# Sums over later keys in a stick-breaking attention: two fp32r passes over a split softplus in place of one native 32 bit pass

## What is computed

```
z = (q . k) / 8                                   # per head, query t, key s
log_beta = log_sigmoid(z);  log_fail = -softplus(z) where s < t, else 0
survive[t, s] = sum of log_fail[t, j] over the keys j later than s
A[t, s] = exp(log_beta[t, s] + survive[t, s]) where s < t, else 0
o = A v
```

## Time and profile before

| | |
|---|---|
| time, median of 3 runs | 875.36 us (873.93 to 876.03) |
| profiled execution: time, span | 875.22 us, 873.3 us |
| TensorE busy | 844.2 us, 97% of the span |
| VectorE busy | 613.9 us, 70% |
| ScalarE busy | 489.5 us, 56% |
| granted TensorE clock, mean | 0.99 |

### The profile page before, as it was taken

How to read it: one execution, slowest core, us unless ns; L and a number is a source line. 1 busy time by engine, 2 the same in 40 slices (tenths; PEclk the granted TensorE clock), 3 DMA queues, 4 the chain that set the end, 5 groups by cost and what they waited for, 6 DMA issues and landing times.

```text
span 873.3 us, 16776 instructions
## 1 busy us (share of the span) xinstructions
PE 844.2 (97%) x6768; PEld 805.1 (92%) x6768; DVE 613.9 (70%) x1004; ACT 489.5 (56%) x814; POOL 145.8 (17%) x151
## 2 busy tenths in 40 slices
PE   7999999999999999999999998899999999999996
PEld 6999999999999989999999988799999999878886
DVE  6646887886666686776764588877797696567754
ACT  6346456455444575555564457768767564345554
POOL 0000000000000333333331121634324010000002
PEclk9999999999999999999999999799999999999999
DMA  9654424335566534555566524544545375653331
GB/s 338 205 158 140 139 98 169 122 125 180 181 190 184 178 97 152 185 180 185 190 193 205 180 88 134 184 153 150 167 148 164 106 235 180 186 168 111 110 95 49
DMA packets 39853, 139.81 MB, mean 160 GB/s; under 512 B 4432, under 2 KB 5600, under 8 KB 39648
## 3 DMA queue, kind: packets, MB, share of 16 engines
q1 hardware_dynamic: 37728, 135.71, 48.8%
q10 hardware_dynamic: 2048, 3.02, 1.0%
HBM read 137.65 MB, written 1.06 MB: 159 GB/s over the span
## 4 chain that ended last, share of the span: by engine, by line
PE 75%; DVE 12%; ACT 7%; issue 3%; POOL 2%; DMA 1%; DVEq 0%; SPq 0%; ACTq 0%; POOLq 0%
PE ps L1582 59%; PE ps L1585 4%; DVE weights_lo L981 4%; PE ps L1607 3%; ACT weights_hi L548 1%; PE ps L1679 1%; DVE arena L1201 1%; DVE arena L1173 1%; PE ps L1669 1%; POOL arena L441 1%; PE ps L1694 1%; DVE arena L1497 1%; ACT arena L923 1%; DVE arena L1248 1%; PE ps L1935 1%
## 5 line engine op out<-in xcount | busy, mean ns | idle before, releaser
L981 DVE TENSOR_TENSOR weights_lo<-raw_weights,weights_hi 128x1024 fp32r<-128x1024 f32 x252 | 312.6, 1244 | 105.5 <-ACT weights_hi L548 105.4
L1582 PE MATMUL ps<-x_hi,weights_hi 128*128 128x256 f32 (+3 forms) x1288 | 375.3, 291 | 7.1 <-DVE weights_lo L981 3.6
L548 ACT ACTIVATE weights_hi<-raw_weights 128x1024 fp32r<-128x1024 f32 x252 | 264.6, 1053 | 181.4 <-issue 82.4
L1582 PE MATMUL ps<-x_lo,weights_hi 128*128 128x256 f32 (+3 forms) x1288 | 365.2, 284 | 0.0
L1582 PE MATMUL ps<-x_hi,weights_lo 128*128 128x256 f32 (+3 forms) x1288 | 364.7, 283 | 0.0
L1582 PEld LDWEIGHTS ps<-x_hi,weights_hi 128*128 128x128 f32 x1288 | 244.9, 190 | 15.1 <-issue 6.7
L1582 PEld LDWEIGHTS ps<-x_lo,weights_hi 128*128 128x128 f32 x1288 | 245.2, 190 | 1.0 <-issue 0.7
L1582 PEld LDWEIGHTS ps<-x_hi,weights_lo 128*128 128x128 f32 x1288 | 245.0, 190 | 0.0
L1582 PE MATMUL ps<-y_hi,weights_hi 128*128 128x256 f32 (+1 forms) x488 | 137.7, 282 | 1.4 <-POOL y_lo L445 1.4
L1582 PE MATMUL ps<-y_lo,weights_hi 128*128 128x256 f32 (+1 forms) x488 | 137.4, 282 | 0.0
L1582 PE MATMUL ps<-y_hi,weights_lo 128*128 128x256 f32 (+1 forms) x488 | 137.2, 281 | 0.0
(11 more groups left out here) (230 smaller groups left out, 1074.3 us busy)
## 6 DMA issues: line engine op xcount, KB each, us to landing
raw_weights<-weights_in SPq DMA_DIRECT2D x252, 512.0 KB, 4.0
arena<-decay_rows ACTq DMA_DIRECT2D x8, 256.0 KB, 4.0
masks<-masks_in SPq DMA_DIRECT2D x1, 1379.0 KB, 11.0
hidden<-xT_in SPq DMA_DIRECT2D x2, 272.0 KB, 3.6
hidden<-xT_in SPq DMA_DIRECT2D x1, 544.0 KB, 6.0
raw_weights<-weights_in SPq DMA_DIRECT2D x2, 256.0 KB, 4.3
out<-arena SPq DMA_DIRECT2D x4, 128.0 KB, 2.2
out<-arena ACTq DMA_DIRECT2D x4, 128.0 KB, 2.1
```

The lines of the kernel that those rows point to most:

```text
L548: a.sig(A(whi[:, s * CW:(s + 1) * CW], raw[:, (c % RAW) * CW:(c % RAW + 1) * CW], ACT.Copy), "hi_ready")
L981: d.sig(TT(wlo[:, s * CW:(s + 1) * CW], raw[:, (c % RAW) * CW:(c % RAW + 1) * CW], whi[:, s * CW:(s + 1) * CW].bitcast(F32), ALU.subtract) ...
L1582: ins = mm(bank(BANK_OF[no])[:, 0:b - a], wt, x_[:, kt, a:b], start=s0, stop=s1)
```

## The change

`fz` is no longer the operand of `survive`. ScalarE copies it, rounded to fp32r, into `f_hi` (`fail_high`, between `att_high(p-1)` and the weight split of b). VectorE writes the remainder into `f_lo` (`fail_low`, between the gated product of line 1104 and `att_low(p-1)`). The two mask matrices are copied to fp32r once, ahead of the first pair. `survive(h)` runs its three matmuls on `f_hi` and then on `f_lo`, each with a wait of its own. The four new tiles lie in a part of the `y_hi` and `y_lo` buffers that is written only later.

```diff
--- before.py
+++ after.py
@@ -199,6 +199,10 @@
         fhi, flo = v3(yhi_t[:, 0:FT * L], FT), v3(ylo_t[:, 0:FT * L], FT)
         ehi, elo = v3(yhi_t[:, 0:16 * L], 16), v3(ylo_t[:, 0:16 * L], 16)
         CONV, ATT, MERGED = 0, 1, 2
+        spare = MERGED * KT * NA
+        f_hi, f_lo = v3(yhi_t[:, spare:spare + 2 * ZC], 2), v3(ylo_t[:, spare:spare + 2 * ZC], 2)
+        later = yhi_t[:, spare + 2 * ZC:spare + 2 * ZC + P]
+        at_or_later = yhi_t[:, spare + 2 * ZC + P:spare + 2 * ZC + 2 * P]
 
         def mask(name):
             o, n = MASKS[name]
@@ -610,6 +614,14 @@
                 if i:
                     take_values_of(i - 1)
 
+            a.sig(A(later, mask("neg_ones"), ACT.Copy), "neg_masks")
+            a.sig(A(at_or_later, mask("neg_tri"), ACT.Copy), "neg_masks")
+
+            def fail_high(p):
+                for e in range(2):
+                    act.wait_ge(S("f_ready"), 2 * p + e + 1)
+                    a.sig(A(f_hi[:, e, :], fz[:, e, :], ACT.Copy), "f_hi")
+
             def softplus_part(p):
                 act.wait_ge(S("z_ready"), p + 1)
                 need(act, "f_ready", 2 * p)
@@ -643,6 +655,7 @@
                 feed(("h", p))
                 if p:
                     att_high(p - 1)
+                fail_high(p)
                 feed(("b", p))
                 act.wait_ge(S("conv_y"), p + 1)
                 a.sig(A(yhi[:, CONV, p, :], bb[:, p % 2, :], ACT.Copy), "conv_hi")
@@ -1055,6 +1068,11 @@
                 d.sig(STT(out=fz[:, h % 2, :], in0=bank(4 + h % 2)[:, 0:ZC], scalar=0.0, in1=mask("stick_neg"),
                           op0=ALU.min, op1=ALU.add), "loga_taken")
 
+            def fail_low(p):
+                for e in range(2):
+                    dve.wait_ge(S("f_hi"), 2 * p + e + 1)
+                    d.sig(TT(f_lo[:, e, :], fz[:, e, :], f_hi[:, e, :].bitcast(F32), ALU.subtract), "f_lo")
+
             def att_low(p):
                 dve.wait_ge(S("att_hi"), p + 1)
                 d.sig(TT(ylo[:, ATT, p, :], bank(6 + p % 2)[:, 0:NA], yhi[:, ATT, p, :].bitcast(F32), ALU.subtract),
@@ -1102,6 +1120,7 @@
                 d.sig(TT(bb[:, p % 2, :], r, rinv[:, TA:T], ALU.mult), "out_taken")
                 d.settle()
                 d.sig(TT(bb[:, p % 2, :], bb[:, p % 2, :], c_, ALU.mult), "conv_y")
+                fail_low(p)
                 if p:
                     att_low(p - 1)
             feed(("b", KT - 1))
@@ -1672,17 +1691,19 @@
 
             def survive(h):
 
-                pe.wait_ge(S("f_ready"), h + 1)
-                zb, f_ = bank(4 + h % 2), fz[:, h % 2, :]
-                later = mask("neg_ones")
+                pe.wait_ge(S("neg_masks"), 2)
+                zb, e = bank(4 + h % 2), h % 2
                 c1, c2 = SEG[1][0], SEG[2][0]
-                mm(zb[:, 0:ZC], mask("neg_tri"), f_, start=False, stop=False, skip_group_check=True)
-                mm(zb[:, 128 - TA:NA], later, f_[:, c1:c2], start=False, stop=False, skip_group_check=True)
-                at = (4 + h % 2) * 512 + 256 - TA
+                at = (4 + e) * 512 + 256 - TA
                 both = ps[:].rearrange("p b c -> p (b c)")[:, at:at + 2 * (c1 + TA - 128)].rearrange(
                     "p (s c) -> p s c", s=2)[:, :, 0:ZC - c2]
-                mm(both, later, f_[:, c2:ZC].unsqueeze(1).to_broadcast([P, 2, ZC - c2]), start=False, stop=True,
-                   skip_group_check=True).then_inc(S("loga_ready"), 1)
+                for n, f_ in enumerate((f_hi[:, e, :], f_lo[:, e, :])):
+                    pe.wait_ge(S("f_lo" if n else "f_hi"), h + 1)
+                    mm(zb[:, 0:ZC], at_or_later, f_, start=False, stop=False, skip_group_check=True)
+                    mm(zb[:, 128 - TA:NA], later, f_[:, c1:c2], start=False, stop=False, skip_group_check=True)
+                    ins = mm(both, later, f_[:, c2:ZC].unsqueeze(1).to_broadcast([P, 2, ZC - c2]), start=False,
+                             stop=n == 1, skip_group_check=True)
+                ins.then_inc(S("loga_ready"), 1)
 
             def attend(p):
                 pe.wait_ge(S("a_ready"), 2 * p + 2)
```

## The result

The changed kernel takes 889.21 us (median of 4 runs, 887.74 to 891.85) against 875.69 us for the kernel before (median of 4 runs; 875.36 was that of three of them): a ratio of 1.0161, 95% interval 1.0133 to 1.0189. It is slower, and inside the range forecast (882 to 893), but 4.3 us above the forecast 884.9. The profiled execution took 889.07 us, with a span of 887.3.

The account below looks back on a forecast made before the run. TensorE bounds the kernel, with `survive` newly waiting on VectorE. Profiled 875.22 us + 8.7 for stands (1.71 + 7 x 1.00) + 0.85 for clock = 884.8; median 0.14 above, so 884.9 us, range 882 to 893.

Parts of the forecast that it names:

- TensorE is the bound, and stands in line with VectorE through the new wait: TensorE, busy 97% of the span, sets the time; `survive` would now wait for VectorE's `fail_low`, put behind line 1104.
- The low part is ready at 111.31, TensorE stands 1.94 us, 2.65 in the first pair: In `survive`, after the first high pass, TensorE waits for the first head's `fail_low`: 1.94 us a pair, 2.65 in the first.
- The loss returns in each pair: The loop from `scores` to `scores` closes, so 1.00 us is lost in each of seven pairs: period 17.09 us against 16.09.
- A pass costs 0.33 us: In `survive`, three rounded matmuls of 418, 144 and 32 columns take 0.19, 0.07 and 0.07 us; a head 0.66 against 1.13.
- the lower bound: Price of `survive`'s narrow rounded matmuls: 0.07 us each for 144 and 32 columns; the upper bound was native cost, 0.25 and 0.14.
- rival 1: In `survive`, narrow rounded matmuls are as slow as native ones: 14.7 us lost, 890.9 us with the 0.85; chance 0.20.
- The clock: even odds of one drop, 0.85 us: TensorE's clock drops at the first stand with even odds, a drop costing 1.7 us, so 0.85; none at the other stands.
- Rival 2: TensorE's clock drops at each stand in the stage, 8 x 1.7 us: 897.6 us; chance 0.12.
- Nothing gives it back after the stage: After the changed stage TensorE goes on without a gap, so the 8.7 us lost there stay lost.
- the likeliest case alone: The forecast with low cost for `survive`'s narrow matmuls, spanning 882 to 888 us; chance 0.60.
- `log_weight` ahead of `scores` stays hidden: VectorE's two `log_weight` end about 114, the next `scores` needs them at 115.4: 1.4 us to spare, no wait.
- The estimate of the other side, 867.9 us: Rival: the low part isn't late for `survive`, TensorE doesn't stand, 7.5 us of work saved shows: 867.9 us; chance 0.05.

Follow-up runs that it names:

- e1: Kernel before plus one wait: TensorE starts `survive` of a head pair only after VectorE's gated product (line 1104), sums native and unsplit; 892.97 us, ratio 1.0204.
- e2: Changed kernel with `survive` native on unsplit `fz`, waiting for `f_ready` alone; `fail_high`, `fail_low` and masks still made but unread; 874.87 us, ratio 0.9994.
- e8: Early remainder version (e3) with `att_low` moved behind the two `log_weight`; 871.13 us, ratio 0.9950 to the kernel before.
- e5: Changed kernel with TensorE's stand filled by native 256 column matmuls, four a pair, five in the first; 886.0 us, ratio 1.0123 to the kernel before.
- e4: Changed kernel with TensorE's passes ordered high, high, low, low in place of high, low, high, low; 885.34 us, ratio 1.0113 to the kernel before.
- e3: Changed kernel with `fail_low` done one head at a time and moved ahead on VectorE; 873.46 us, ratio 0.9979 to the kernel before.
- e7: Changed kernel with `fail_low` taken out of VectorE and done by GpSimd; 877.09 us, ratio 1.0022 to the kernel before.
- e6b: Changed kernel with `fail_low` moved two instructions earlier, ahead of the scaled b result; 877.9 us, ratio 1.0029 to the kernel before.

## Why the prediction came out as it did

**TensorE is the bound, and stands in line with VectorE through the new wait: right.** e1 has the wait without the split and is slower still; e2 has the work without the wait and costs nothing.

**The low part is ready at 111.31, TensorE stands 1.94 us, 2.65 in the first pair: right, to 0.02 us.** Counted as the prediction counts, from the start of the first pass plus its 0.33, the stands are 1.92 and 2.64 us (98.37 to 100.29, 77.36 to 80.00). The profile's 1.76 and 2.48 count from a matmul's modelled end, 0.16 later. VectorE's part was right to 0.1 us (remainder 0.34 us behind the start of the gated product, two of them in 1.09).

**The loss returns in each pair: right.** The periods are equal to 0.01 us, but for those with a slow clock; 17.35 measured, 17.09 predicted.

**A pass costs 0.33 us: this term was too small.** The first pass of a pair does cost 0.33; behind another pass it is 0.42. I had priced each matmul by itself and taken the lower bound. For 144 and 32 columns that bound was right (0.07 each), so rival 1 falls. But the 418 column matmul behind a 32 column one takes 0.28 start to start, not the 0.19 that it takes behind a 258 column one. What I had left out is the rate of the weight loads, and my reason for it was a misreading of the rows before: 0.14 us is the distance of two starts of matmuls, while the loads for them start earlier and further apart. Timeline of the weight loads (PEld) of the kernel before, at the native 32 columns (line 1684) and the 418 behind them, then of the changed kernel, one pass and the first load of the next:

```profile
109.93 0.31 PEld L1684 LDWEIGHTS ps<-arena,masks 128*128 128x128 f32 x2
110.16 0.30 PEld L1679 LDWEIGHTS ps<-arena,masks 128*128 128x128 f32 x2
...
100.69 0.19 PEld L1702 LDWEIGHTS ps<-y_hi 128*128 128x128 f32 x1
100.81 0.19 PEld L1703 LDWEIGHTS ps<-y_hi 128*128 128x128 f32 x1
101.00 0.19 PEld L1704 LDWEIGHTS ps<-y_hi 128*128 128x128 f32 x1
101.11 0.19 PEld L1702 LDWEIGHTS ps<-y_lo,y_hi 128*128 128x128 f32 x1
```

The two native loads take 110.16 - 109.93 = 0.23 us, not 0.14, and from 95 to 205 us no two loads of 128 columns start less than 0.10 us apart in either kernel. In the changed kernel a pass is 0.12 + 0.19 + 0.11 = 0.42 from load to load. The Trainium skill's rule on weight loads ("TensorE: Matmul & The Clock Gate", section "LDWEIGHTS (loading the stationary operand)"), which I had turned down because of the native pair's row, gave 0.41 for the pass. The runs bear out its sum for a pass behind another, though the time shows at the wide matmul and not at the narrow ones. Three passes a pair, 0.26 us, 2.1 us over eight pairs. By it the saving on TensorE is 8 x 0.69 = 5.5 us (e8: 16.09 - 15.41 = 0.68 a pair), not 7.5.

**The clock: even odds of one drop, 0.85 us: too small.** In the profiled execution it fell twice, which cost 1.07 us in the first pair's passes (2.33 us for 1.26) and 1.86 and 1.55 us in "c": 4.5 us, which e5 confirms. I had priced a drop at 1.7 us, from one that lasted 3.4 us. The second drop lasted as long and cost 1.55, near that price; the first lasted 6.8 us and cost 2.93, and the forecast's sum had room for neither a second drop nor a longer one. In e1 and e4 the drop in the first pair lasted 3.4 us. Rival 2, a drop at each stand, didn't come.

**Nothing gives it back after the stage: nearly right.** 1.2 us came back outside the stage, for which the clock in the second block is the likely cause. It comes and goes between versions (e5 lost most of it again), so I don't count it as the change's.

The sum then: 8.7 + 2.1 (passes) + 4.5 (clock) - 1.2 = 14.1 us, for 13.9 measured between the profiled executions. Both misses, the passes and the clock, point the same way: 889.2 lies above the 888 that the likeliest case alone was to span. It is inside the range by the room made for rival 1, which did not come, so that the range held is partly luck.

**`log_weight` ahead of `scores` stays hidden: right for the changed kernel, and wrong as soon as its stand is gone** (e3, e7). The estimate of the other side, 867.9 us, had left it out; what could be had was 871.1.

**Left open:** why one stand of 1.76 us in seven let the clock fall, and why the first drop lasted twice as long as in e1 and e4; and how often the drops occur, though the changed kernel's runs (887.74 to 891.85) spread wider than those of the kernel before (873.93 to 876.32), and the slowest has a mean clock of 0.987 for 0.991 in the profiled one.

## What to carry to other kernels

Ask of a split that is to make matmuls cheaper where its second half is computed, and by when the matmul wants it: here work that costs nothing by itself (e2) cost 14 us by its place in one engine's order, and gained 4 once moved (e8). If such a chain closes on itself from one iteration to the next, its lateness is paid in each, and the stand also puts the clock at risk. When one wait is removed, compute the next one in the same loop; and price a row of short matmuls by a row of short matmuls, not one by one.

## What was not expected of the hardware

A 418 column fp32r matmul costs 0.19 us start to start behind a 258 column one and 0.28 behind a 32 column one, with the loads of 128 columns of weights never closer than 0.10 us. A GpSimd subtraction of 1.08 us stretched a VectorE product with two SBUF operands from 0.60 to 1.44 us. And the clock in this stage: stands of 1.46 and 1.49 us left it at full speed (e4, e6b), behind those of 2.17, 2.40 and 2.48 us it fell to 1.2 GHz, once each (first pair of e4, e1, changed kernel), and behind one of fourteen of 1.68 to 1.78 us (changed kernel and e1). A fall lasted 3.4 us or 6.8, and began between 0.3 us before TensorE resumed and 1.9 us after.
